# The low parts of the weights, made in four GpSimd instructions of 512 columns a slot instead of one of 2048

## The reference

```python
for layer in range(2):                      # first block
    x = x + 0.5 * rms_norm(swiglu(rms_norm(x), w_ffn_in, w_ffn_out))      # stages F0, F2
    x = x + rms_norm(mixer(rms_norm(x)))    # layer 0: mLSTM (MI, MO); layer 1: differential attention (DQ, DO)
    x = x + 0.5 * rms_norm(swiglu(rms_norm(x), w_ffn_in, w_ffn_out))      # F1, F3
    x = x + rms_norm((p @ w_ple_proj) * sigmoid(rms_norm(x) @ w_ple_gate))   # P0, P1
    # after layer 0: the shared keys and values (KV)
u = rms_norm_2(x)                           # second block, "hybrid"
proj = u @ w_in                             # HI, 10240 columns: convolution, attention, gates
y_conv = (silu(zc) * bg * conv(cg * xc)) @ w_out_conv                       # HC
y_attn = (silu(za) * mixture_of_dilations(q, k, v)) @ w_out_attn            # HA
out = rms_norm_2(x + (g_conv * y_conv + g_attn * y_attn) @ w_o)             # HO
```

## Time and profile before

| | |
|---|---|
| median of three runs | 1462.7 us (1462.68 to 1465.63) |
| the profiled execution's own time | 1466.3 us |
| its span, first to last instruction | 1464.4 us |
| mean granted TensorE clock | 0.979 |
| TensorE busy with matmuls | 1389.5 us, 95% of the span |
| GpSimd busy | 1037.0 us, 71% |
| ScalarE busy | 659.1 us, 45% |
| VectorE busy | 495.7 us, 34% |

### The profile page before, as it was taken

How to read it: one execution, slowest core, us unless ns; L and a number is a source line. 1 busy time by engine, 2 the same in 40 slices (tenths; PEclk the granted TensorE clock), 3 DMA queues, 4 the chain that set the end, 5 groups by cost and what they waited for, 6 DMA issues and landing times.

```text
span 1464.4 us, 17488 instructions
## 1 busy us (share of the span) xinstructions
PE 1389.5 (95%) x6396; PEld 1136.8 (78%) x6396; DVE 495.7 (34%) x1108; ACT 659.1 (45%) x760; POOL 1037.0 (71%) x241
## 2 busy tenths in 40 slices
PE   6799999989999999999999789999999999989997
PEld 4588888777888878888887567888878777778786
DVE  5610124565110156211003675110156133572235
ACT  5344435436444445544434556343455443544531
POOL 5778885818978866888887408978866966658763
PEclk9899999999999999999999989999999999999999
DMA  8555554515665554565655405556554644436541
GB/s 260 172 181 186 183 190 158 181 62 188 193 195 186 184 174 166 185 217 173 192 180 201 134 1 182 188 191 199 173 180 150 199 149 141 141 118 205 191 144 51
DMA packets 160668, 246.94 MB, mean 169 GB/s; under 512 B 8892, under 2 KB 99812, under 8 KB 160484
## 3 DMA queue, kind: packets, MB, share of 16 engines
q1 hardware_dynamic: 158180, 238.90, 49.9%
q10 hardware_dynamic: 2432, 7.28, 1.4%
HBM read 245.10 MB, written 1.05 MB: 168 GB/s over the span
## 4 chain that ended last, share of the span: by engine, by line
PE 36%; POOL 33%; issue 23%; DVE 5%; ACT 1%; DMA 1%; POOLq 1%; SPq 0%; ACTq 0%; DVEq 0%
POOL w_lo L502 33%; PE acc L1583 6%; PE acc L1585 6%; PE acc L1584 6%; PE gu L1583 3%; PE gu L1584 3%; PE gu L1585 3%; PE acc L1610 1%; PE acc L1616 1%; PE acc L1613 1%; PE gu L1958 1%; ACT w_hi L533 1%; DMA w_raw<-in_w_ffn_in 1%; PE tb L1967 1%; PE tb L1583 0%
## 5 line engine op out<-in xcount | busy, mean ns | idle before, releaser
L502 POOL TENSOR_TENSOR w_lo<-w_raw,w_hi 128x2048 fp32r<-128x2048 f32 x224 | 1031.5, 4623 | 396.2 <-ACT w_hi L533 389.0
L533 ACT CAST w_hi<-w_raw 128x2048 fp32r<-128x2048 f32 x226 | 425.9, 1907 | 78.7 <-PE gu L1585 20.8
L1583 PE MATMUL gu<-w_hi,xT_hi 128*128 128x512 f32 x832 | 331.7, 399 | 3.4 <-DVE xT_lo L1015 3.4
L1584 PE MATMUL gu<-w_lo,xT_hi 128*128 128x512 f32 x832 | 326.2, 392 | 0.0
L1585 PE MATMUL gu<-w_hi,xT_lo 128*128 128x512 f32 x832 | 326.1, 392 | 0.0
L1583 PE MATMUL acc<-w_hi,xT_hi 128*128 128x512 f32 x544 | 220.6, 406 | 3.7 <-DVE xT_lo L1015 2.7
L1585 PE MATMUL acc<-w_hi,xT_lo 128*128 128x512 f32 x544 | 214.8, 395 | 0.0
L1584 PE MATMUL acc<-w_lo,xT_hi 128*128 128x512 f32 x544 | 214.3, 394 | 0.0
L1583 PEld LDWEIGHTS gu<-w_hi,xT_hi 128*128 128x128 f32 x832 | 157.8, 190 | 35.4 <-issue 3.6
L1585 PEld LDWEIGHTS gu<-w_hi,xT_lo 128*128 128x128 f32 x832 | 157.6, 189 | 33.7
L1584 PEld LDWEIGHTS gu<-w_lo,xT_hi 128*128 128x128 f32 x832 | 158.0, 190 | 31.5 <-issue 0.2
(11 more groups left out here) (299 smaller groups left out, 1258.5 us busy)
## 6 DMA issues: line engine op xcount, KB each, us to landing
w_raw<-in_w_ffn_in SPq DMA_DIRECT2D x176, 512.0 KB, 4.7
w_raw<-in_w_ffn_out SPq DMA_DIRECT2D x88, 512.0 KB, 4.2
w_raw<-in_w_in SPq DMA_DIRECT2D x80, 512.0 KB, 4.5
w_raw<-in_mlstm_w_in SPq DMA_DIRECT2D x24, 512.0 KB, 4.3
w_raw<-in_w_ple_gate SPq DMA_DIRECT2D x16, 512.0 KB, 4.3
w_raw<-in_w_kv SPq DMA_DIRECT2D x16, 512.0 KB, 4.4
w_raw<-in_mlstm_w_out SPq DMA_DIRECT2D x8, 512.0 KB, 4.3
w_raw<-in_diff_w_q SPq DMA_DIRECT2D x8, 512.0 KB, 4.0
```

The lines of the kernel that those rows point to most:

```text
L502: pool.tensor_tensor(w_lo[:, slot.spl, :], w_raw[:, slot.raw, :], w_hi[:, slot.spl, :].bitcast(F32), ALU.subtract).then_inc(lo_ready, 1)
L533: nc.scalar.copy(w_hi[:, slot.spl, :], w_raw[:, slot.raw, :]).then_inc(hi_ready, 1)
L1583: mm(out, xh, wh, start=(half == 0 and k == 0), stop=False)
L1584: mm(out, xh, wl, start=False, stop=False)
```

## The change

GpSimd's function `subtract` makes the low part of a slot in four instructions, each on 512 of the 2048 columns, in order. It waits once ahead of the first for the cast, and the last of the four increments `lo_ready`. The half slot at L507 and the two instructions of VectorE are as they were. Nothing else differs.

```diff
+PART = 512
...
             def subtract(slot):
                 pool.wait_ge(hi_ready, slot.count())
-                pool.tensor_tensor(w_lo[:, slot.spl, :], w_raw[:, slot.raw, :],
-                                   w_hi[:, slot.spl, :].bitcast(F32), ALU.subtract).then_inc(lo_ready, 1)
+                for part in range(SLOT // PART):
+                    cols = slice(PART * part, PART * part + PART)
+                    ins = pool.tensor_tensor(w_lo[:, slot.spl, cols], w_raw[:, slot.raw, cols],
+                                             w_hi[:, slot.spl, cols].bitcast(F32), ALU.subtract)
+                ins.then_inc(lo_ready, 1)
```

## The result

The kernel takes 1451.2 us in the median of 4 runs (1447.3 to 1454.0), against 1463.8 for the kernel before beside it. The ratio is 0.991 (95% interval 0.989 to 0.993). Measured two more times, it was 0.991 (0.990 to 0.993) both times. The forecast was 1453, faster.

A forecast was written before the change was run, and what follows sets the result against it. TensorE was taken as the bound, losing time to waits for VectorE instructions held up by GpSimd's, and to half clock afterwards. Gains of 4.3, 1.6 and 4.7 less 0.2 and 0.6 made 9.8 us: 1453, range 1447 to 1461.

The forecast's parts named there:

- GpSimd's price: GpSimd's slots: 0.05 us per added instruction, bounds 0 and 0.13; a slot in 4.72 us, about 1065 us busy.
- VectorE and GpSimd alternate: Wherever VectorE meets GpSimd's pieces: each VectorE instruction waits for one piece, about 1.18 us, instead of a whole slot.
- rival B: Port between pieces: not freed, VectorE waits for the whole slot as now, only the price is left; 1463.3 us, chance 0.10.
- Tables in F0: L1501 to L1514, ahead of a TensorE wait: thirteen instructions alternate with pieces, end at 52.6 to 53.2; gain 4.3, bounds 1 and 6.
- mLSTM, first place: L1160 waits one piece, so the 2.66 us wait before L1786 disappears; gain 1.6 us, bounds 0.3 and 2.7.
- the step on L1802: mLSTM, first place: small VectorE instructions now meet GpSimd's longer run, cost up to two pieces, and L1802 waits, about 1 us.
- Second place: mLSTM, L987: waits one piece, but three successors each meet another; -0.2 us, bounds -0.5 and +1.1.
- Hybrid: L1373 to L1425 before L1993: TensorE's wait of 4.28 shrinks by 2.7, plus 2.0 of clock; gain 4.7, bounds 2 and 6.
- Tail: Last four slots: L1482 shortens but L1630 waits for matmuls; four slots at +0.15 lose 0.6 us, bounds 0.2 and 1.6.
- The sum: Whole kernel: 4.3 + 1.6 - 0.2 + 4.7 - 0.6 = 9.8 us, giving 1453 us; chance 0.62.
- Rival A: More VectorE instructions meet pieces than counted, and the hybrid stage's clock still falls; gain 2.8 us, 1460 us, chance 0.15.
- C: From 0.34 us per added instruction a slot takes 5.6 us and GpSimd bounds the FFNs; 1464 us, 1508 at 0.45; chance 0.08.

The follow-up runs named there:

- tables-only kernel: Only slots 2 to 11, where VectorE builds the tables of F0, cut in pieces, all others whole as before the change: 1460.0 us, 0.997 of the kernel before.
- kernel with three places: Only slots 2 to 11, 42 to 47 and 198 to 209 cut in pieces, all others whole as before the change: 1453.4 us, ratio 0.992.
- linked kernels: Changed kernel with GpSimd waiting for each piece's semaphore before the next: four pieces per slot 1456.1 us, 0.993; eight pieces 1581.6 us, 1.079.

## Why the prediction was right, point by point

**GpSimd's price: mis-sized.** It took 0.05 us per added instruction with bounds 0 and 0.13; measured 0.14, just beyond. A slot costs 5.00, not 4.72, and GpSimd 1131, not 1065. The step that was off is the 4.62 us of a whole slot: this is the recorded mean, in which successive instructions overlap, where slots in a row start 4.57 apart. The half slot at L507, which runs alone, was nearly a fair witness: in the kernel of two pieces a half came every 2.35 us against its 2.34. The other row, 4.55 for one slot, gave 0.13 and was nearer. The second estimate of the prediction, 1.17 us a piece, was as low, against 1.25. It did little harm, because slots are ready ahead in most stages: TensorE's waits for L505 outside the tail are 0.4 us twice.

**VectorE and GpSimd alternate: right 51 times, wrong once.** In the profiled execution 52 VectorE instructions took over 0.12 us more than the shortest with the same operation, shape and operands in any of the runs; all but one got in at the first boundary. That one, L1486, is the case named at the end of the prediction ("longer than 2.3 us, a wait isn't one piece"), and rival B (the port isn't freed between pieces) was true for it alone. In the two further profiles of this kernel none of 52 was passed over. The steps for chains hold.

**Tables in F0: gain 4.3, measured 4.8.** TensorE resumed 3.15 us earlier in the profiled execution. The forecast end of 52.6 to 53.2 was 54.29. Of this, 0.65 is the later first instruction (35.96), which is no fault of the step; the chain itself took 18.33 us instead of 17.9, the price of the dearer pieces. Against it, the stretch at the lower clock behind the wait is shorter (3.4 us instead of 5.5, by the granted clock near 0.5 in both), which would be worth 1.0 and which the sum had left out. But in the kernel with pieces in the tail only, the same program as before up to here, that stretch was 2.9 us, so this 1.0 isn't shown to come from the change. 4.8 is the tables-only kernel's ratio, 3.1 to 6.6 by its interval; there the first table instruction came amid a piece, the chain ended at 53.18, as forecast, and TensorE resumed at 54.14.

**mLSTM, first place: gain 1.6, measured about 1.9.** From the end of the wait behind the tables to the end of the wait before L1634 (L1630 before), the tables-only kernel takes 252.2 us and the one with three places 250.3. The wait of 2.66 went, and the new one before L1806 is 1.50 (2.28 in the kernel with three places), as the step on L1802 said. **Second place: -0.2**, right in that next to nothing changes: TensorE's wait there is 4.28 us instead of 4.49, so +0.2, within the bounds.

**Hybrid: gain 4.7, measured 7.6, beyond the bound of 6.** The mechanism was right, and one assumption was not: that the slots keep their place against VectorE's work. ScalarE's casts and the activation ahead of the second one, in the kernel before and then after:

```profile
1275.54 1.91 ACT L533 CAST w_hi<-w_raw 128x2048 fp32r<-128x2048 f32 x1
...
1284.48 0.80 ACT L822 ACTIVATE arena<-arena 128x128 f32<-128x128 f32 x2 [7.03 <-DVE arena L1368]
...
1285.54 1.91 ACT L533 CAST w_hi<-w_raw 128x2048 fp32r<-128x2048 f32 x1
```

```profile
1273.10 0.80 ACT L826 ACTIVATE arena<-arena 128x128 f32<-128x128 f32 x2 [4.56 <-DVE arena L1372]
...
1274.17 1.92 ACT L537 CAST w_hi<-w_raw 128x2048 fp32r<-128x2048 f32 x1
...
1280.39 0.92 DVE L1377 CUSTOM_DVE_ANT_0 arena<-arena,times 128x128 f32<-128x128 f32 x1
...
1281.97 0.34 DVE L1417 TENSOR_SCALAR arena<-arena,gcol 128x256 f32<-128x256 f32 x1
```

TensorE is 8.89 us earlier at the start of the stretch, so the cast of 1285.54 "should" come at 1276.65. It comes at 1274.17, 2.5 us sooner still. A likely reason, which no run isolates, is that the head before (L1373 of 3.02 us and L1413 of 4.26 at 1274 to 1282 in the kernel before) is no longer late, and ScalarE's queue with it: the activation ahead of the cast waited 7.03 us for VectorE's L1368, which stands behind those two, and waits 4.56 now. GpSimd's slot is then nearly over when L1377 comes, and L1417 and its successors run free. So TensorE's wait did not shrink by 2.7 us but vanished, and all 3.4 us of clock came back instead of 2.0.

**Tail: loss 0.6, measured 1.7 or 4.2, beyond the bound of 1.6.** Each half of the step was mis-sized: the price (4 x 0.43 = 1.7 us for four slots, which is all of the smaller loss), and the clause that "L1630 behind it waits for matmuls", which presumes that L1482 gets shorter.

**The sum.** 4.8 + 1.9 + 7.6 - 1.7 or 4.2 makes 12.6 or 10.1 us; measured are 0.0089 x 1464, 13.0 us. The errors had both signs: hybrid 2.9 too low, tail 1.1 to 3.6 too optimistic. That 1453 came so near is therefore in part luck, though the mechanism held at every place but the tail. What the sum didn't reckon is the clock away from these places. TensorE's busy time fell from 1389.5 to 1382.0 us for the same work, so more than half of the gain in the two profiled executions is matmuls that ran at full clock, and the mean granted clock was 0.977 to 0.983 in the runs of the kernel before and 0.984 to 0.988 in those of the changed one. The hybrid place explains 3.4 us of it; for the rest no run shows the cause. Rival A (alternation eats the gain) fell at the hybrid stage, C (a dear piece) at 0.14 against its 0.34.

## What to carry to other kernels

Cutting a GpSimd instruction that reads SBUF shortens what VectorE waits for it to one piece, at 0.14 us a cut. It pays where a VectorE chain that TensorE waits for meets GpSimd, and where GpSimd has slack. A chain alternates with the pieces one for one, so it gains only as long as it ends before GpSimd's run does: two pieces instead of one gained nothing for the chain of thirteen. The hand-over between pieces can't be relied on: where GpSimd has many pieces queued and VectorE's result is due soon, leave the slots whole. (Instructions of VectorE with an operand in PSUM showed no such waits here; moving one there wasn't tried.) Where a stretch has several such chains, reckon that removing an early wait moves the other engines' work as well, and don't take the late ones' positions from the old trace.

## What was unexpected about the hardware

With one exception, a VectorE instruction that met a run of GpSimd instructions got in at the first boundary, or it was passed over until GpSimd stopped. In both executions with eight pieces and the one with the long wait in the tail, the waits over several pieces (1.3, 2.0, 11.9, 13.5, 15.9 and 36.7 us among them, twelve in all) ended with GpSimd's run, except one of 2.94 us at L1377, which got in 7 us before that run's end. GpSimd's next instruction begins while the last ends (the records overlap by 0.04 to 0.06 us). In the linked kernels 0.08 us stand between two pieces, and none of the 125 VectorE instructions that waited there waited for more than one piece. Which meetings go wrong is only half settled: L1458 and L1470, which both times waited equally long, were issued in the last 0.1 us of a piece, but L1486 was issued 0.18 us after a piece's start both when it took 9.61 us and when it took 2.2.

The Trainium skill, page "SBUF — State Buffer", section "Who interferes with whom", has the shared ports locked for a whole instruction of the engine that came first. The runs agree as to the lock: one piece, 1.2 us, is the usual wait. They show besides that the end of an instruction need not be the end of the lock for the one that waits. That fits the Trainium skill, page "GPSIMD Engine Reference", section "2.1 Instruction dispatch", by which GpSimd's cores start the next instruction each on its own; no run here looks at the cores one by one.
